# Output projection of a decoder layer: plain float32 products replaced by three products of high and low parts, with split weights stored in DRAM and streamed back

## The chip, the cores and the metric

One core of a Trainium2 chip runs one program. The metric is the device time of one execution in microseconds. The engines are TensorE (PE, with its weight loads as PEld), VectorE (DVE), ScalarE (ACT), GpSimd (POOL) and SyncE (SP), which here issues nearly all DMAs.

## What is computed

Two decoder layers on 1040 tokens (16 meta tokens and 1024 others) of width 1024. The part that matters is the mixer of layer 0. It has eight heads of sparse attention (each query keeps 256 keys) and eight heads of a gated linear recurrence. Their outputs are put side by side and mapped by one matrix:

```
o = jnp.concatenate([o_a.reshape(B, L, A_WIDTH), o_b.reshape(B, L, B_VAL_WIDTH)], axis=-1)
return o @ w_out
...
h = layer_norm(ALPHA * h + mix, ln_mix_g[layer], ln_mix_b[layer])
```

`o` is 1040 x 1024 and `w_out` 1024 x 1024, both float32.

## The kernel before

The program has three stages with a barrier after each: `projection` (to about 464 us), `mixers` (to about 937 us) and `trunk` (the rest: both feed-forward parts, the pooling mixer, the norms).

**Projection.** Most products of this kernel are already made from parts: a float32 operand is rounded to the type float32r (the high part, by ACT), the rest (the low part, by POOL or DVE) is a second float32r tensor, and low x high, high x low and high x high are summed in PSUM. `w_in` comes in twelve slabs of 256 columns. ACT makes `slabH`, POOL makes `slabL` (`split`, L374), PE runs 24 matmuls for each output unit (L498, L501), and ACT takes the unit out of its bank (`out_of_bank`). Slabs 0 and 1 fill gaps of the score computation; slabs 2 to 11 follow. Beside them DVE and ACT search the top 256 keys, and POOL, after its last slab, makes the distances for which DVE then waits. The order of all this is one list, `order`, walked by every engine.

**Mixers.** There are nine tiles m = 0 to 8, the first of 16 tokens, the others of 128. Each tile has eight steps h = 0 to 7, one for each attention head and for one level of the recurrence; after tile 8 come eight steps of m = 9 and six of m = 10 for what is left over. Every engine walks the same list `steps`. On PE a step is, in this order: the logits of head h (`qk`, L1246; it needs the maximum of the head before, `nmax`, from DVE), one level product (`gram`, L1289; it needs POOL's `carry` of the level before, L1124 and L1128), one job on the bank SHARED (`shared_job`), the transposes of the probabilities of the head before (L1303), their product with the values (L1314), and at some steps a quarter of an output projection (`out_job`, `quarter`, L1239). The jobs on SHARED, at steps 0 to 6, are: meta, out, kT, state, qa, ot_att, ot_rec. kT transposes the keys of the recurrence, and ACT copies them to `k_tok` (L1439), after the exponential of the step (L1372) and two gate functions (L1402, L1404). ot_att and ot_rec transpose the outputs of attention and recurrence; ACT copies them to `oT` (L1454, L1450). All users of SHARED follow each other in one count: each waits until the one before has been taken out (`shared_done`).

A quarter is the product of a tile of `oT` with 256 columns of `w_out`: eight plain float32 matmuls, which the chip runs as 16. Its weights lie in `w_out_part`, two halves of 512 KB, each with one buffer. SP asks for the next first half when PE has read the present one (`wq_read`) and for the next second half when the quarter is complete (`load_w`, L1005). DVE adds the result to `y` (`out_added`, L1595). The quarters 0 to 3 of tile t run at (t+1, 7), (t+2, 1), (t+2, 3) and (t+2, 5):

```
jobs = {7: (m - 1, 0), 1: (m - 2, 1), 3: (m - 2, 2), 5: (m - 2, 3)}
```

The last six quarters (two of tile 7 and all of tile 8) take their weights from four 1 MB loads into `kaT` and `va`, which are free at the end (`kept_quarter`, L1046). Those of tile 8 use four banks of their own. DVE finishes the recurrence's output `on` with two products at step 4 (L1635, L1638).

Of the kernel before, what the change touches and what calls it, by code (L numbers as in the profile page):

```python
# [5 lines left out]
F32 = mybir.dt.float32  # L6
# [26 lines left out]
PG = D // len(POOL_WINDOWS)  # L33

# [49 lines left out]
def build(nc, ins, out):  # L84
# [3 lines left out]
    with ExitStack() as top:  # L88
# [21 lines left out]

        banks = top.enter_context(nc.psum_tensor("banks", [P, 8, 512], F32))
# [9 lines left out]
        with ExitStack() as heads:  # L121
            with ExitStack() as mixer:

                score = (y[:, :, :].rearrange("p m d -> p (m d)")[:, NT * D - SC_LAST:NT * D],
                         last_draw)
                kiT = sb(mixer, "kiT", [P, 2, P])
                masks = kiT[:, :, :].rearrange("p a t -> p (a t)").bitcast(U8).rearrange("p (l t) -> p l t", t=P)
                w_qa0 = y[:, 2, :].rearrange("p (k f) -> p k f", k=QC)
                kaT = sb(mixer, "kaT", [P, 4, L])
                va = sb(mixer, "va", [P, NT, A_WIDTH])  # L130
                with stage() as c:
                    projection(nc, c, sem, sb, banks, ident, x, meta, w_in_v, ins, score, cqT, kaT, va, y, qz_dram, vg_dram, kiT, masks, w_qa0)
                with stage() as c:
                    mixers(nc, c, sem, sb, banks, ident, x, meta, ins, score, masks, w_qa0, cqT, kaT, va, y, qz_dram, vg_dram, raw, draw)
            hH = sb(top, "hH", [P, DC, L], F32R)
            hL = sb(top, "hL", [P, DC, L], F32R)
# [4 lines left out]
def projection(nc, c, sem, sb, banks, ident, x, meta, w_in_v, ins, score, cqT, kaT, va, y, qz_dram, vg_dram, kiT, masks, w_qa0):  # L141
# [26 lines left out]
    slab_in_va = va[:, :, :].rearrange("p m f -> p (m f)")[:, 0:2 * SLAB].rearrange("p (s k f) -> p s k f", s=2, k=DC)  # L168

# [45 lines left out]
    dist_done, placed = sem("dist_done"), sem("placed")  # L215
    stored = [sem(f"stored{i}") for i in range(NS)]
# [43 lines left out]

    def slab_part(n):
# [46 lines left out]
    def _(sp):  # L308
        for m, (t0, n) in enumerate(TILES):
# [12 lines left out]
            if m == 2:  # L322
# [8 lines left out]
                sp.dma_start(w_qi[:, :, :], ins["w_uq_idx"][0].rearrange("(k p) f -> p k f", p=P)).then_inc(w_qi_loaded, 16)  # L331
        for j, (col, _, _, _) in enumerate(SLABS):
# [5 lines left out]
            if j == len(SLABS) - 2:  # L338
                sp.wait_ge(sc_psum, len(units))
            sp.dma_start(slab_raw(j), w_in_v[:, :, col:col + SW]).then_inc(slab_loaded[j % 2], 16)  # L340
            if j == len(SLABS) - 2:
                sp.dma_start(w_qa0, ins["w_uq"][0].rearrange("(k p) f -> p k f", p=P)).then_inc(w_qa_loaded, 16)

    @block.gpsimd
    def _(pool):
# [39 lines left out]
        for what, m, *part in order:  # L385
# [15 lines left out]
            elif what == "low":  # L401
                split(m)
                splits += 1
        pool.wait_ge(qi_psum, 2 * NQ)
# [102 lines left out]
    def _(act):  # L507
# [35 lines left out]
        for what, m, *part in order:  # L543
            if what == "split":
                split(m)
            if what == "out":
# [245 lines left out]
def mixers(nc, c, sem, sb, banks, ident, x, meta, ins, score, masks, w_qa0, cqT, kaT, va, y, qz_dram, vg_dram, raw, draw):  # L792
# [44 lines left out]
    oT = sb(c, "oT", [P, 2, DC, P])  # L837
    QW = D // 4
    wq = sb(c, "w_out_part", [P, 2, DC // 2, QW])
# [19 lines left out]
    op_psum, op_added = sem("op_psum"), sem("op_added")  # L859
# [26 lines left out]
    def out_job(m, h):  # L886

        jobs = {7: (m - 1, 0), 1: (m - 2, 1), 3: (m - 2, 2), 5: (m - 2, 3)}
# [4 lines left out]

    def kept_quarter(t, q):

        return t == NT - 1 or (t == NT - 2 and q in LAST_ORDER[0:2])
# [60 lines left out]

    block = c.enter_context(nc.Block())

    @block.sync  # L960
    def _(sp):
# [36 lines left out]
        def load_w(job):  # L998
            for kh in range(2):
# [4 lines left out]
                q = job % 4  # L1004
                sp.dma_start(wq[:, kh, :, :], w_v[:, kh * 4:kh * 4 + 4, q * QW:(q + 1) * QW]).then_inc(wq_loaded[kh], 16)  # L1005

# [20 lines left out]
        for m, h in steps:  # L1027
# [143 lines left out]
    def _(pe):  # L1171
# [56 lines left out]
        def quarter(m, q, bank):  # L1228
            n = TILES[m][1]
            for k in range(DC):  # L1230
                if kept_quarter(m, q):
                    w = wq_last[q][:, k, :]
                    if k == 0:
                        pe.wait_ge(wl_loaded[q], 16)
                else:
                    w = wq[:, k // 4, k % 4, :]
                    if k % 4 == 0:
                        pe.wait_ge(wq_loaded[k // 4], 16 * (4 * m + q + 1))
                last = nc.tensor.matmul(banks[0:n, bank, 0:QW], oT[:, m % 2, k, 0:n], w, start=(k == 0), stop=(k == DC - 1))  # L1239
# [123 lines left out]
    def _(act):  # L1363
# [59 lines left out]
        def off_shared(what, m):  # L1423
# [25 lines left out]
            if what == "ot_rec":  # L1449
                ins_ = nc.scalar.activation(oT[:, m % 2, 4:8, 0:n], four(src)[:, :, P - n:P], ACT.Copy)  # L1450
            if what == "ot_att":
                if m >= 2:
                    act.wait_ge(shared_psum, nth["op", m - 2, 3])
                ins_ = nc.scalar.activation(oT[:, m % 2, 0:4, 0:n], four(src)[:, :, 0:n], ACT.Copy)  # L1454
# [32 lines left out]
    def _(dve):  # L1487
# [111 lines left out]

        gates(0, 4)  # L1600
        nc.vector.memset(S[:], 0.0).then_inc(dve_pads, 1)
        for i, (m, h) in enumerate(steps):
# [11 lines left out]
            if 1 <= i <= NU:  # L1614
                turned(i - 1)
            if out_job(m, h):
# [817 lines left out]
```

## Time and profile before

| | us |
|---|---|
| median of 3 runs (lowest, highest) | 2550.95 (2549.44, 2551.99) |
| the profiled execution, its own time | 2547.58 |
| its span, first to last instruction | 2545.9 |
| PE busy | 2469.9 (97%) |
| DVE, ACT, POOL busy | 1114.2, 950.1, 1062.1 |
| mean granted TensorE clock | 0.992 of full speed |

The profiled execution took 1.7 us more than its span. Busy time of PE says that matmuls were under way, not that they ran at their fastest, since they overlap; the start of one instruction to the start of the next tells what one costs. An idle time in brackets stands before an instruction and names what ended it.

### The profile page before, as it was taken

To read this page: it belongs to the slowest core of one execution; us is meant where nothing else is said; L and a number is where in the kernel's file an instruction comes from. 1 tells how busy PE (TensorE), PEld (TensorE's weight loads), DVE (VectorE), ACT (ScalarE), POOL (GpSimd) and SP (SyncE) were. 2 spreads that over 40 slices of the span, in tenths; PEclk is the share of its full clock that TensorE was granted. 3 is DMA by queue.
4 is the path that set the end of the run, shared out by engine and by line. 5 is a ranking of instruction groups with operands and counts; after the bars stand their busy time and mean duration, and the time that the engine had idled before them with its cause. 6 is when DMAs were issued, how large, how long until landed. Compare 5 with 4: busy or idle time off the path is not lost.

```text
span 2545.9 us, 36095 instructions
## 1 busy us (share of the span) xinstructions
PE 2469.9 (97%) x14044; PEld 2129.0 (84%) x14044; DVE 1114.2 (44%) x2233; ACT 950.1 (37%) x1609; POOL 1062.1 (42%) x617
## 2 busy tenths in 40 slices
PE   7999999899999989999999999999999999999997
PEld 7889999768888778899898888888888888888885
DVE  7798986444554523333333332333323322232224
ACT  3687783334443224222223332323333322332222
POOL 1434213365554224444433544544434443455342
PEclk9999999899999999999999999999999999999998
DMA  4101230333332333333323323333233233333431
GB/s 139 34 18 56 79 103 24 108 112 110 113 106 90 93 116 109 96 96 105 89 74 99 99 75 93 88 112 97 70 99 100 67 116 99 100 89 110 116 94 47
DMA packets 275002, 231.43 MB, mean 91 GB/s; under 512 B 10768, under 2 KB 255568, under 8 KB 274832
## 3 DMA queue, kind: packets, MB, share of 16 engines
q1 hardware_dynamic: 266640, 220.59, 29.1%
q10 hardware_dynamic: 8192, 8.52, 1.0%
q8 instruction: 113, 1.85, 0.3%
q14 instruction: 57, 0.47, 0.1%
HBM read 215.81 MB, written 12.71 MB: 90 GB/s over the span
## 4 chain that ended last, share of the span: by engine, by line
PE 60%; ACT 1%; DVE 1%; DMA 1%; POOL 0%; issue 0%; POOLq 0%; SPq 0%; ACTq 0%; DVEq 0%
PE banks L2067 38%; PE banks L2101 19%; PE banks L2137 1%; PE banks L2115 1%; PE banks L1764 1%; PE banks L2124 1%; PE banks L2092 0%; PE banks L2095 0%; DMA last_draw<-in_w_down 0%; DMA cq_raw<-in_w_up 0%; POOL dL L1985 0%; POOL wL L1978 0%; DVE y L2318 0%; ACT dH L2187 0%; ACT hH L1774 0%
## 5 line engine op out<-in xcount | busy, mean ns | idle before, releaser
L1978 POOL TENSOR_TENSOR wL<-cq_raw,wH 128x2048 fp32r<-128x2048 f32 x87 | 407.0, 4678 | 531.5 <-ACT wH L2181 531.5
L2067 PE MATMUL banks<-hL,wH 128*128 128x512 f32 (+1 forms) x1760 | 618.7, 352 | 6.6 <-ACT hid L2196 3.8
L2067 PE MATMUL banks<-hH,wL 128*128 128x512 f32 (+1 forms) x1760 | 617.9, 351 | 0.0
L2067 PE MATMUL banks<-hH,wH 128*128 128x512 f32 (+1 forms) x1760 | 616.2, 350 | 0.0
L2292 DVE TENSOR_TENSOR hid<-hid,banks 128x512 f32<-128x512 f32 (+1 forms) x110 | 64.4, 585 | 729.4 <-PE banks L2067 629.0
L2067 PEld LDWEIGHTS banks<-hL,wH 128*128 128x128 f32 x1760 | 331.3, 188 | 55.8 <-ACT hid L2196 5.1
L2067 PEld LDWEIGHTS banks<-hH,wL 128*128 128x128 f32 x1760 | 331.2, 188 | 46.3
L2067 PEld LDWEIGHTS banks<-hH,wH 128*128 128x128 f32 x1760 | 331.8, 188 | 45.0
L1985 POOL TENSOR_TENSOR dL<-last_draw,dH 128x1024 fp32r<-128x1024 f32 x88 | 220.9, 2510 | 321.3 <-ACT dH L2187 321.2
L2318 DVE TENSOR_TENSOR y<-y,banks 128x512 f32<-128x512 f32 (+1 forms) x340 | 232.3, 687 | 195.0 <-PE banks L2101 194.0
L2187 ACT ACTIVATE dH<-last_draw 128x1024 fp32r<-128x1024 f32 x88 | 93.3, 1061 | 517.6 <-PE banks L2101 340.7
L2101 PE MATMUL banks<-dH,hidL 128*128 128x512 f32 x704 | 279.2, 397 | 2.3 <-issue 2.3
L2101 PE MATMUL banks<-dL,hidH 128*128 128x512 f32 x704 | 278.0, 395 | 0.0
L2101 PE MATMUL banks<-dH,hidH 128*128 128x512 f32 x704 | 277.5, 394 | 0.0
L2198 ACT ACTIVATE hidH<-hid 128x512 fp32r<-128x512 f32 (+1 forms) x110 | 60.4, 549 | 382.1 <-DVE hid L2292 382.1
L2181 ACT ACTIVATE wH<-cq_raw 128x2048 fp32r<-128x2048 f32 x87 | 166.0, 1908 | 40.1 <-DMA cq_raw<-in_w_up 37.8
L2101 PEld LDWEIGHTS banks<-dH,hidL 128*128 128x128 f32 x704 | 132.3, 188 | 35.0 <-issue 2.7
L2101 PEld LDWEIGHTS banks<-dH,hidH 128*128 128x128 f32 x704 | 132.6, 188 | 31.5
L1124 POOL TENSOR_TENSOR qp<-qp,tot 64x256 f32<-64x256 f32 x112 | 80.6, 720 | 186.9 <-PE banks L1289 182.5
L2101 PEld LDWEIGHTS banks<-dL,hidH 128*128 128x128 f32 x704 | 132.6, 188 | 30.5
L501 PE MATMUL banks<-shared,hH 128*128 128x256 f32 (+1 forms) x648 | 136.9, 280 | 0.0
L501 PE MATMUL banks<-shared,hL 128*128 128x256 f32 (+1 forms) x432 | 120.7, 280 | 0.0
(279 smaller groups left out, 4124.4 us busy)
## 6 DMA issues: line engine op xcount, KB each, us to landing
cq_raw<-in_w_gate SPq DMA_DIRECT2D x88, 512.0 KB, 4.5
cq_raw<-in_w_up SPq DMA_DIRECT2D x88, 512.0 KB, 6.0
last_draw<-in_w_down SPq DMA_DIRECT2D x88, 512.0 KB, 3.4
w_out_part<-in_w_out SPq DMA_DIRECT2D x60, 512.0 KB, 3.9
va<-in_w_in SPq DMA_DIRECT2D x10, 1024.0 KB, 5.4
va<-in_x SPq DMA_DIRECT2D x8, 512.0 KB, 4.3
vg_scratch<-y ACTq DMA_DIRECT2D x32, 128.0 KB, 1.7
y<-in_x SPq DMA_DIRECT2D x8, 512.0 KB, 7.5
```

The lines of the kernel that those rows point to most:

```text
L501: last = nc.tensor.matmul(banks[0:n, bank, 0:SW], h[:, k, a:a + n], w[:, k, :], start=first, stop=stop)
L1124: nc.gpsimd.tensor_tensor(late, late, blocks[r, :, 0, :].to_broadcast([HD, n, 2 ** l]), ALU.mult)\
L1764: last = self.nc.tensor.transpose(self.banks[:, self.bank_of(i), k * P:k * P + n], self.y[0:n, m, kk * P:(kk + 1) * P], self.ident[0:n, 0:n])
L1978: nc.gpsimd.tensor_tensor(wL[:, ff % 2, :, :, :].rearrange("p g k f -> p (g k f)"), raw[:, :, :, :].rearrange("p g k f -> p (g k f)"), wH[ ...
L1985: nc.gpsimd.tensor_tensor(dL[:, ff % 2, :], draw, dH[:, ff % 2, :].bitcast(F32), ALU.subtract)\
L2067: last = nc.tensor.matmul(banks[:, GU + (2 * q + g) % 3, 0:n], wt[:, ff % 2, g, k, :], h[:, k, a:a + n], start=(k == 0 and part == 0), sto ...
L2101: last = nc.tensor.matmul(banks[0:n, DN + num % 3, :], h[:, (2 * g + u) % 3, t0 - ph.t0:t0 - ph.t0 + n], wt[:, u, (j % 2) * 512:(j % 2 + 1 ...
L2181: nc.scalar.activation(wH[:, ff % 2, :, :, :], raw[:, :, :, :], ACT.Copy).then_inc(w_hi, 2)
L2187: nc.scalar.activation(dH[:, ff % 2, :], draw, ACT.Copy).then_inc(d_hi, 1)
L2198: nc.scalar.activation(hidH[:, ff % 3, a - ph.t0:a - ph.t0 + n], hid[:, q % 2, 0:n], ACT.Copy)\
L2292: nc.vector.tensor_tensor(hid[:, q % 2, 0:n], hid[:, q % 2, 0:n], banks[:, GU + (2 * q + 1) % 3, 0:n], ALU.mult)\
L2318: nc.vector.tensor_tensor(at, at, banks[0:n, DN + num % 3, :], ALU.add).then_inc(y_added, 1)
```

## The change

The quarters of tiles 0 to 7 become three float32r products for each of the eight pieces: 24 matmuls. Only tile 8 stays plain. The copy of `oT` becomes `oH` by ACT and `oL` by DVE (`o_low`), both with one buffer. In the projection stage eight pieces of `w_out` (512 KB each) are loaded, split by ACT (128 x 1024) and POOL, and both parts are written to the DRAM tensor `w_out_split` in pieces of 1 MB; SP issues this beside slabs 5 to 9. The mixers stream 1 MB for each half, for all 32 quarters. The quarters move to the steps 7, 1, 2 and 4. `oT` of tile 8 lies in `probs`.

```diff
@@ projection, order list
+    OUT_WITH = 5
+    split_after = [first_unit[OUT_WITH - 3 + c // 2] + 2 + c % 2 * 2 for c in range(len(OUT_CHUNKS))]
...
         if k == DC - 1:
             order.append(("out", u))
+            if u in split_after:
+                order.append(("w_out", split_after.index(u)))
@@ projection, SP
+        def load_out(c):
+            q, kh = OUT_CHUNKS[c]
+            if c >= 2:
+                sp.wait_ge(wo_stored[c % 2], 16 * (c // 2))
+            sp.dma_start(out_part(c)[:, 1, :].rearrange("p (k f) -> p k f", k=DC // 2),
+                         w_out_v[:, 4 * kh:4 * kh + 4, q * QW:(q + 1) * QW]).then_inc(wo_loaded[c % 2], 16)
+
+        def store_out(c):
+            q, kh = OUT_CHUNKS[c]
+            sp.wait_ge(wo_lo, c + 1)
+            sp.dma_start(wo_dram[q, kh], out_part(c)).then_inc(wo_stored[c % 2], 16)
...
             if j == len(SLABS) - 2:
-                sp.wait_ge(sc_psum, len(units))
+                for i in range(2):
+                    sp.wait_ge(wo_stored[i], 16 * len(OUT_CHUNKS) // 2)
             sp.dma_start(slab_raw(j), w_in_v[:, :, col:col + SW]).then_inc(slab_loaded[j % 2], 16)
...
+            for c in range(2 * (j - OUT_WITH) - 2, 2 * (j - OUT_WITH)):
+                if 0 <= c < len(OUT_CHUNKS):
+                    store_out(c)
+                if j >= OUT_WITH and c + 2 < len(OUT_CHUNKS):
+                    load_out(c + 2)
@@ mixers
-    oT = sb(c, "oT", [P, 2, DC, P])
-    wq = sb(c, "w_out_part", [P, 2, DC // 2, QW])
+    oH = sb(c, "oH", [P, DC, P], F32R)
+    oL = sb(c, "oL", [P, DC, P], F32R)
+    wq = sb(c, "w_out_part", [P, 2, 2, DC // 2, QW], F32R)
+    oT_last = probs[:, :, 0:DC // 2 * P].rearrange("p a (k t) -> p a k t", k=DC // 2)
...
-        jobs = {7: (m - 1, 0), 1: (m - 2, 1), 3: (m - 2, 2), 5: (m - 2, 3)}
+        jobs = {7: (m - 1, 0), 1: (m - 2, 1), 2: (m - 2, 2), 4: (m - 2, 3)}
@@ mixers, SP
-                sp.dma_start(wq[:, kh, :, :], w_v[:, kh * 4:kh * 4 + 4, q * QW:(q + 1) * QW]).then_inc(wq_loaded[kh], 16)
+                sp.dma_start(wq[:, kh, :, :, :].rearrange("p a k f -> p a (k f)").bitcast(F32), wo_dram[job % 4, kh]).then_inc(wq_loaded[kh], 16)
...
-                if t < NT - 1 and 4 * t + q + 1 < 4 * (NT - 1) - 2:
+                if 4 * t + q + 1 < 4 * (NT - 1):
                     load_w(4 * t + q + 1)
@@ mixers, PE, quarter
+                for part, (o, w) in enumerate(((oL, 0), (oH, 1), (oH, 0))):
+                    last = nc.tensor.matmul(banks[0:n, bank, 0:QW], o[:, k, 0:n], wq[:, k // 4, w, k % 4, :],
+                                            start=(k == 0 and part == 0), stop=(k == DC - 1 and part == 2))
@@ mixers, ACT, off_shared
+                    if m:
+                        act.wait_ge(shared_psum, nth["op", m - 1, 3])
+                    nc.scalar.activation(oH[:, 4 * half:4 * half + 4, 0:n], o_columns(what, n), ACT.Copy).then_inc(o_hi, 1)
@@ mixers, DVE
+        def o_low(what, m):
...
+            dve.wait_ge(o_hi, 2 * m + half + 1)
...
+            nc.vector.tensor_tensor(oL[:, at, 0:n], o_columns(what, n), oH[:, at, 0:n].bitcast(F32), ALU.subtract)\
+              .then_inc(shared_done, 1)
```

The instructions move at three places. First PE at tile 7, steps 2 to 4, before (L1193 is kT, L1196 state, L1185 qa):

```order
L1193 MATMUL banks<-ident,key 128x128 x4
L1303 MATMUL banks<-ident,probs 128x128 x7
L1314 MATMUL banks<-va,pT 128x64 x7
L1246 MATMUL banks<-kaT,qaT 128x512
L1246 MATMUL banks<-kaT,qaT 128x400
L1289 MATMUL banks<-qp,key 128x128 x4
L1196 MATMUL banks<-vt,k_tok 128x128 x4
L1303 MATMUL banks<-ident,probs 128x128 x7
L1314 MATMUL banks<-va,pT 128x64 x7
L1239 MATMUL banks<-w_out_part,oT 128x256 x8
```

and the same place now (every line number of this part is 46 to 48 higher; the quarter is L1286):

```order
L1239 MATMUL banks<-ident,key 128x128 x4
L1351 MATMUL banks<-ident,probs 128x128 x7
L1362 MATMUL banks<-va,pT 128x64 x7
L1286 MATMUL banks<-w_out_part,oL 128x256
L1286 MATMUL banks<-w_out_part,oH 128x256 x2
...
L1294 MATMUL banks<-kaT,qaT 128x512
L1294 MATMUL banks<-kaT,qaT 128x400
L1337 MATMUL banks<-qp,key 128x128 x4
L1242 MATMUL banks<-vt,k_tok 128x128 x4
```

The quarter stood behind the state job, a step later; now it is the next user of SHARED behind kT.

Then DVE at tile 8, steps 4 to 6, now (L1648 is `out_added`, L1698 and L1701 finish `on`, L1562 the maxima, L1658 the new low part):

```order
L1648 SCALAR_TENSOR_TENSOR y<-y,banks 128x256
L1698 TENSOR_TENSOR on<-on,rsh 128x512
L1701 TENSOR_TENSOR on<-on,gt 128x512
L1562 ISA probs,nmax<-banks,last_draw 128x1024
...
L1585 COPY pT<-banks 128x512
L1658 TENSOR_TENSOR oL<-banks,oH 128x512
L1736 BN_STATS n_bn<-y 128x6
L1737 BN_STATS n_bn<-y 128x6
```

Before, `out_added` of the last quarter stood at the place of the first L1658, a step later, and DVE had no low parts to make.

Last, SP at the end of the mixers, before and now:

```order
L1046 DMA kaT<-in_w_out 128x8x256 x2
L1046 DMA va<-in_w_out 128x8x256 x2
L1058 DMA last_draw<-in_w_down 128x1024
```

```order
L1051 DMA w_out_part<-w_out_split 128x2048 x2
L1092 DMA kaT<-in_w_out 128x8x256 x2
L1051 DMA w_out_part<-w_out_split 128x2048 x2
L1092 DMA va<-in_w_out 128x8x256 x2
L1051 DMA w_out_part<-w_out_split 128x2048 x2
L1104 DMA last_draw<-in_w_down 128x1024
```

Two pairs of streamed halves now stand between and behind the loads of the last tile's weights.

## Rows read from the trace of the kernel before

**Rows 1.** The page's busy time, and busy time in a stretch of the mixers.
```profile
PE 2469.9 (97%) x14044; PEld 2129.0 (84%) x14044; DVE 1114.2 (44%) x2233; ACT 950.1 (37%) x1609; POOL 1062.1 (42%) x617
...
600.00:700.00 100.00, 99.82 (x675) 86.94 (x674) 51.82 (x107) 41.23 (x104) 54.11 (x70) 1.00 0.38 116
```
**Rows 2.** Timeline of PE, tile 5, steps 1 to 4: start, length, engine, line, instruction.
```profile
670.99 3.62 PE L1239 MATMUL banks<-w_out_part,oT 128*128 128x256 f32 x16
674.44 1.27 PE L1246 MATMUL banks<-kaT,qaT 128*128 128x512 f32 x4
...
678.50 1.32 PE L1246 MATMUL banks<-kaT,qaT 128*128 128x512 f32 x4
...
683.35 3.67 PE L1239 MATMUL banks<-w_out_part,oT 128*128 128x256 f32 x16
686.85 1.27 PE L1246 MATMUL banks<-kaT,qaT 128*128 128x512 f32 x4
```
**Rows 3.** Timeline of ACT in the projection: copies that follow a unit of 24 products.
```profile
417.66 0.38 ACT L526 ACTIVATE va<-banks 128x256 f32<-128x256 f32 x1 [2.44 <-PE banks L501]
420.50 0.38 ACT L526 ACTIVATE va<-banks 128x256 f32<-128x256 f32 x1 [2.46 <-PE banks L501]
```
**Rows 4.** Timeline of ACT, tile 5, step 2: gate functions, then the keys.
```profile
678.93 0.61 ACT L1402 ACTIVATE u<-zt 128x512 f32<-128x512 f32 x1
...
680.11 0.58 ACT L1439 ACTIVATE k_tok<-banks 128x512 f32<-128x512 f32 x1
```
**Rows 5.** Timelines of PE and ACT: the same place in tiles 2 and 7.
```profile
538.27 0.68 PE L1246 MATMUL banks<-kaT,qaT 128*128 128x272 f32 x2
539.46 0.58 ACT L1439 ACTIVATE k_tok<-banks 128x512 f32<-128x512 f32 x1
...
789.23 1.75 PE L1246 MATMUL banks<-kaT,qaT 128*128 128x512 f32 x4
790.23 0.58 ACT L1439 ACTIVATE k_tok<-banks 128x512 f32<-128x512 f32 x1
```
**Rows 6.** PE's waits in step 3: tile 2's product, and the waits list, 480 to 940.
```profile
539.99 1.13 PE L1289 MATMUL banks<-qp,key 128*128 128x128 f32 x8 [1.04 <-POOL key L1128]
...
PEld banks L1196 <- ACT k_tok L1439: 1.1, 3, 0.5
```
**Rows 7.** Timelines of POOL (tile 5) and DVE (tile 5, and the end).
```profile
694.54 1.72 POOL L1124 TENSOR_TENSOR qp<-qp,tot 64x256 f32<-64x256 f32 x2
...
693.42 1.64 DVE L1638 TENSOR_TENSOR on<-on,gt 128x512 f32<-128x512 f32 x1
...
917.22 0.69 DVE L1638 TENSOR_TENSOR on<-on,gt 128x512 f32<-128x512 f32 x1
```
**Rows 8.** The page's DMA issues (size, median to landing), and the landings of kaT.
```profile
last_draw<-in_w_down SPq DMA_DIRECT2D x88, 512.0 KB, 3.4
w_out_part<-in_w_out SPq DMA_DIRECT2D x60, 512.0 KB, 3.9
va<-in_w_in SPq DMA_DIRECT2D x10, 1024.0 KB, 5.4
...
DMA to landing us min/median/max: 6.7/7.9/9.1
```
**Rows 9.** Timeline of PE at the end of the mixers.
```profile
906.34 3.62 PE L1239 MATMUL banks<-w_out_part,oT 128*128 128x256 f32 x16
910.54 3.72 PE L1239 MATMUL banks<-kaT,oT 128*128 128x256 f32 x16 [0.58 <-DVE y L1595]
...
917.00 3.72 PE L1239 MATMUL banks<-kaT,oT 128*128 128x256 f32 x16 [1.50 <-ACT oT L1454]
921.31 0.66 PE L1217 MATMUL banks<-ident,on 128*128 128x128 f32 x4 [0.58 <-DVE y L1595]
922.65 7.17 PE L1239 MATMUL banks<-kaT,oT 128*128 128x256 f32 x32 [0.69 <-ACT oT L1450]
```
**Rows 10.** Timeline of DVE in the projection, after its search.
```profile
422.11 1.03 DVE L755 TENSOR_SCALAR_CACHE_REDUCE search_rows<-y,found 128x784 f32<-128x784 f32 x1 [19.70 <-POOL y L409]
```

More of the change, by code:

```diff
@@ L33 @@
 PG = D // len(POOL_WINDOWS)
+QW = D // 4
+OUT_CHUNKS = [(q, kh) for q in range(4) for kh in range(2)]
 COL_CQ, COL_KA, COL_VA = 0, Q_RANK, Q_RANK + A_WIDTH
@@ L403, in _ @@
                 splits += 1
+            elif what == "w_out":
+                pool.wait_ge(wo_hi, m + 1)
+                low = out_part(m)[:, 1, :]
+                nc.gpsimd.tensor_tensor(low.bitcast(F32R), low, out_part(m)[:, 0, :], ALU.subtract).then_inc(wo_lo, 1)
         pool.wait_ge(qi_psum, 2 * NQ)
@@ L545, in _ @@
                 split(m)
+            if what == "w_out":
+                act.wait_ge(wo_loaded[m % 2], 16 * (m // 2 + 1))
+                nc.scalar.activation(out_part(m)[:, 0, :].bitcast(F32R), out_part(m)[:, 1, :], ACT.Copy).then_inc(wo_hi, 1)
             if what == "out":
@@ L789, in _, with mixers @@
         linked(nc.vector.tensor_scalar(masks[:, LEVELS, :], xor, 0.0, None, ALU.is_equal))
-def mixers(nc, c, sem, sb, banks, ident, x, meta, ins, score, masks, w_qa0, cqT, kaT, va, y, qz_dram, vg_dram, raw, draw):
+def mixers(nc, c, sem, sb, banks, ident, x, meta, ins, score, masks, w_qa0, cqT, kaT, va, y, qz_dram, vg_dram, wo_dram, raw, draw):
     W = 4 * P
@@ L956, in four, with o_columns @@
         return ap.rearrange("p (f t) -> p f t", f=4)
+    def o_columns(what, n):
+        return four(banks[:, SHARED, :])[:, :, P - n:P] if what == "ot_rec" else four(banks[:, SHARED, :])[:, :, 0:n]
     block = c.enter_context(nc.Block())
@@ L1448, in off_shared @@
                 ins_ = nc.scalar.activation(on[:, :], src, ACT.Copy)
[L1449 to L1454, printed above, removed]
+            if what in ("ot_att", "ot_rec"):
+                half = what == "ot_rec"
+                if m == NT - 1:
+                    act.wait_ge(meta_kept, NU)
+                    act.wait_ge(t_psum, turned_to(NU - 1))
+                    ins_ = nc.scalar.activation(oT_last[:, half, :, :], four(src), ACT.Copy)
+                else:
+                    if m:
+                        act.wait_ge(shared_psum, nth["op", m - 1, 3])
+                    nc.scalar.activation(oH[:, 4 * half:4 * half + 4, 0:n], o_columns(what, n), ACT.Copy).then_inc(o_hi, 1)
+                    return
             ins_.then_inc(shared_done, 1)
@@ L1598, in out_added @@
                 dve.wait_ge(shared_done, nth["op", m, 3])
+        def o_low(what, m):
+            n = TILES[m][1]
+            half = what == "ot_rec"
+            dve.wait_ge(o_hi, 2 * m + half + 1)
+            at = slice(4 * half, 4 * half + 4)
+            nc.vector.tensor_tensor(oL[:, at, 0:n], o_columns(what, n), oH[:, at, 0:n].bitcast(F32), ALU.subtract)\
+              .then_inc(shared_done, 1)
         gates(0, 4)
@@ L1615, in _ @@
                 turned(i - 1)
+            if shared_job(m, h) and shared_job(m, h)[0] in ("ot_att", "ot_rec") and m < NT:
+                o_low(*shared_job(m, h))
             if out_job(m, h):
```

35 lines of the change are left out of this document (20 added, 15 removed).

## The prediction

> **What bounds the kernel now.** Read the page first: PE is busy for 97% of the span, and in the middle of the mixers for 99.8 of 100 us, while DVE and POOL are at half [rows 1]. That alone doesn't say that shorter products shorten the stage, so the timeline of PE comes next. In tile 5 each step starts where the one before ends, with no idle time to speak of [rows 2]: there PE's own work sets the pace. The second thing to see is how late the others run behind it. ACT finishes k_tok at 680.69, when PE has been in the next step since 678.50 [rows 2, 4]. That lateness is free now, because PE first needs k_tok after its logits and level product of step 3. The third view is the end of the mixers, where PE waits between quarters [rows 9] and loads stand behind each other [rows 8].
>
> **The product itself.** A plain quarter takes from 670.99 to 674.44, 3.45 us, and at step 3 from 683.35 to 686.85, 3.50 us [rows 2]; I take 3.45. A unit of 24 float32r products of the same shape, 128 x 256, takes 420.50 − 417.66 = 2.84 us in the projection [rows 3]. So a quarter loses 0.61 us. 28 quarters lie before the end piece, which is worked out by itself: 28 x 0.61 = **−17.1 us**, if PE keeps the pace.
>
> **The move of quarter 2 to step 2.** It now stands directly behind kT on SHARED and can't start before k_tok is copied. The copy comes late for a reason that the change leaves alone: it starts from quarter 1 of the same tile, after which DVE adds, normalizes and takes the maximum, and ACT does the exponential, two gates, then the copy [rows 4]. In tile 5 PE arrives at the quarter at 678.50 and the copy ends at 680.69, 0.07 us of signal more: 2.26 us of wait. In tile 2 it is 540.04 against 538.27, 1.84 us; in tile 7 790.81 against 789.23, 1.65 us [rows 5]. The three between (3, 4, 6) read 2.34, 2.35 and 1.95 in the same way. Six tiles: **+12.4 us**. In tile 8 the copy comes in time, since PE there waits for DVE anyway. Something comes back: behind this wait PE no longer waits in step 3 for POOL (1.04 us in tile 2) or for k_tok (1.1 us in three places) [rows 6], nor for some 0.25 us of others: **−2.4 us**. The bounds are 0 (were PE to arrive as late as the copy) and the full 12.4.
>
> **The low part and DVE's queue.** `o_low` is one DVE instruction of 128 x 512, twice a tile, 0.69 us by the nearest row of that size, 917.22 [rows 7]. DVE has room on average, but look at what is queued behind one wait: at step 4 `out_added` now waits for quarter 3, and behind it stand the two products on `on`, the maximum of step 5, the low part, four statistics instructions and the maximum of step 6, while PE has two steps without a quarter (692.24 − 686.85 = 5.4 us was step 4; a step without special jobs in tile 5 is 678.50 − 674.44 = 4.1 us [rows 2]). From the end of quarter 3 DVE needs 0.3 + 0.3 + 1.3 to 2.9 + 1.0 + 0.6 + 0.2 + 0.7 + 1.7 + 0.8 = 6.9 to 8.5 us before the maximum of step 6 is there; PE wants it after two steps, at 8.2 us. The spread is `on`: 1.64 us for one product beside POOL, 0.69 us alone [rows 7]. POOL is likely idle at that moment now, because it had all of quarter 3 to finish. I take +0.4 us a tile, 7 tiles, **+3 us**, with the ends 0 and 1.5 us a tile (10 us). The Trainium skill (SBUF — State Buffer, "SBUF: two separate sides") says that a DVE instruction with two SBUF inputs and a GpSimd instruction exclude each other for a whole instruction. By that rule the doubling is a wait for POOL, the trace agrees, and this term would be near its low end where POOL is idle.
>
> **Short steps.** Steps 3 and 5 lose their quarter. POOL needs 1.72 us for the first two instructions of a level [rows 7] and 0.63 for the third, so a step must be about 3.3 us or PE waits at its level product, as it does in tile 2 [rows 6]. In tiles 2 and 3 steps 3 and 5 fall to some 2.5 to 3.6 us. With the copies of qa before quarter 3, **+2 us** (0 to 4).
>
> **Weights.** Each half is now 1 MB. A 1 MB load landed after 5.4 us; 512 KB after 3.9 with rows of 1 KB and 3.4 with rows of 4 KB [rows 8]. The new pieces are rows of 8 KB, so I take 4.7 for one and 2.7 more for one queued behind (the two kaT loads, issued 0.5 us apart, landed 2.4 us apart after issue, 2.9 us apart in time [rows 8]). The tight place is quarter 1 to 2. The first half is asked for 1.4 us before quarter 1 ends and lands 3.3 us after its end; the second lands about 6 us after its end. PE wants them at 2.6 + 1.8 = 4.4 us and 5.9 us in tile 2 and later in the others. The wait for k_tok covers them: **+0.5 us**. If that cover were gone, they would cost about what it costs. The Trainium skill (DMA: Bandwidth & Descriptors, "Measured") gives 6.15 us for 1 MB; by it tile 2 alone would wait longer, and the end piece below would be some 3 us longer. The row of 5.4 us is this kernel's, so it is preferred.
>
> **The end.** Before, quarters 2 and 3 of tile 7 had kept weights; they ran at 910.54 and 917.00, the second behind ot_att, and the last four quarters began at 922.65 [rows 9]. Now (9,1), (9,2) and (9,4) hold nothing on PE but three quarters, each needing a fresh pair of 1 MB halves in buffers that are just being read, and two pairs of 1 MB loads share the queue. By the rates above: quarter 1 ends near 908.5. Its successor's first half is asked for at 907.1, behind two kaT loads that now end near 908.2, and lands at 911.7, the second at 914.5: quarter 2 ends at 915.9. The va pair, issued meanwhile, is through at 920.3; the halves of quarter 3 follow at 923.0 and 925.6, and it ends at 927.0. Then ot_att and ot_rec, one after the other, each with a transpose of 0.66, a copy and 0.6 us of waits: 3.5 us. The last four quarters start at 930.5 instead of 922.65: **+7.9 us** (5 to 11).
>
> **The projection stage.** Eight ACT copies (half of a slab's 1.9 us each) and eight POOL subtractions (half of 4.6 us) are added, and sixteen DMAs on SP. The ACT copies, and whatever they cost DVE, fall on the search, which ends 19.7 us before POOL lets DVE go on [rows 10]; PE's output banks are eight deep. SP's new waits (for the low part, for a store) lie about a slab ahead of the next slab load. I cost it at **0**; without that cover the copies would cost up to 8 us.
>
> Sum: −17.1 + 12.4 − 2.4 + 3 + 2 + 0.5 + 7.9 = **+6.3 us**. On the profiled execution's 2547.6 this is 2553.9; that execution lies 3.4 us under the median, so I forecast 2550.95 + 6.3 = **2557 us**.
>
> **Rivals.** (1) *The waits are mostly absorbed, the product wins.* PE's wait at step 2 gives DVE, ACT and POOL a lead, and later waits vanish: half of the 12.4 is paid, no DVE or short-step term, end +5: −17.1 + 6.2 − 2.4 + 5 = −8, 2543 us. For it: DVE and POOL are half idle. Against: the bracketed waits of PE that could vanish are few. (2) *Everything small comes out well but the two big waits stay*: −17.1 + 12.4 − 2.4 + 7.9 = +0.8, 2552 us, no change. (3) *Weights become the bound at quarter 2.* Loads in company took 6.7 to 9.1 us [rows 8]. From a second half that lands more than 5.9 us (tile 2) to 8.2 us (tile 7) after quarter 1's end, PE waits for it instead of k_tok; at 9.1 us this adds 3.2, 1.9, 1.6, 1.4, 1.1, 0.9: +10 us, 2567 us. Against: little other traffic stands at step 1. (4) *The split isn't hidden in the projection*: SP, blocked on a store, delays a slab, or ACT's copies delay a unit: +8 us, 2565 us. Against: the slack above.
>
> **Numbers.** The measurement tells about 0.2%, 5.1 us, from no change. Forecast and its neighbourhood (2553 to 2561): 0.4; rival 2: 0.2; rival 1: 0.2; rival 3: 0.12; rival 4: 0.08. Faster by over 0.2% (under 2545.9) is rival 1 and a little: 0.2. Rival 2 and the lower third of the forecast give no change (to 2556.1): 0.33. The rest is slower: 0.47. The range takes in rival 1's time and ends at rival 3's: 2543 to 2567.
>
> **What would show it.** Right: quarters of 2.8 us on PE; a wait of about 2 us before quarter 2 in tiles 2 to 7, ended by ACT's k_tok; two gaps of several us, ended by DMAs into w_out_part, before the second and third of the three quarters near 910; the projection's end still at 464. Wrong: gaps before quarter 2 ended by w_out_part (rival 3), a later barrier (rival 4), PE waits for DVE's maxima at steps 6 and 7 much over 0.4 us a tile, or quarters that take over 3 us, which would take away the gain on which all of it stands.

## The result, and the profile after

The change makes the kernel slower: 2575.1 us median (2571.19 to 2576.3, 4 runs) against 2550.26 (2549.44 to 2551.99, 4 runs), a ratio of 1.0094 with a 95% interval of 1.0078 to 1.0110. That is +24.8 us where +6.3 was forecast, and above the upper end of the range. The two profiled spans are 2574.6 and 2545.9 us, mean granted clock 0.983 and 0.992.

The page of the changed kernel, busy time and DMA issues, and two stretches, of which the second answers to [rows 1]:

```profile
PE 2468.5 (96%) x14300; PEld 2144.0 (83%) x14300; DVE 1121.2 (44%) x2249; ACT 955.7 (37%) x1617; POOL 1078.6 (42%) x625
...
w_out_part<-w_out_split SPq DMA_DIRECT2D x64, 1024.0 KB, 5.3
...
va<-in_w_in SPq DMA_DIRECT2D x10, 1024.0 KB, 5.9
w_out_split<-slab_last SPq DMA_DIRECT2D x8, 1024.0 KB, 8.6
...
slab_last<-in_w_out SPq DMA_DIRECT2D x8, 512.0 KB, 4.2
```
```profile
300.00:400.00 100.00, 92.39 (x726) 90.30 (x726) 79.36 (x232) 77.07 (x141) 27.11 (x8) 0.97 0.41 135
600.00:700.00 100.00, 94.90 (x713) 85.19 (x712) 48.61 (x108) 39.53 (x102) 52.98 (x70) 0.96 0.54 195
```

The first of these windows lies in the projection, and read before the change:

```profile
300.00:400.00 100.00, 100.00 (x830) 97.99 (x829) 82.23 (x248) 78.80 (x150) 18.49 (x4) 1.00 0.25 82
```

PE is busy 1.4 us less than before in a span that is 28.7 us longer: PE is idle for longer, in the projection and in the mixers. The clock column fell too, from 1.00 to 0.97 and 0.96, so part of the busy time is at half speed and hides how much shorter the products have become. Over the whole trace the granted clock is at half (1.2 GHz) for 45 us before and for 89 us now.

**Where the 28.7 us lie.** DVE's first instruction of the mixers marks the end of the projection. Before:

```profile
464.62 0.48 DVE L1495 MEMSET key<- 128x512 f32 x1 [11.37 <-PEq L101]
```

and now:

```profile
479.30 0.48 DVE L1548 MEMSET key<- 128x512 f32 x1 [10.34 <-PEq L103]
```

The mixers begin 14.7 us later. POOL's first mask instruction, which stands ahead of everything that the change adds, already starts at 199.91 us where it was 196.48; so 3.4 of the 14.7 us are of this execution's start, and 11.3 of the projection. For the rest each trace is divided at three marks (the first quarter, the end of tile 7's quarter 1, the start of the last four quarters), with the time that the clock was at half:

| us | before | changed |
|---|---|---|
| start of the mixers, less what the start is late | 464.6 | 475.9 |
| first quarter to the end of tile 7's quarter 1 | 390.5 | 390.9 |
| of it with PE idle | 7.5 | 20.5 |
| of it with the clock at half | 0 | 14 |
| from there to the last four quarters | 12.7 | 24.6 |
| mixers as a whole | 473.9 | 485.1 |

**The projection** has three waits on PE where there was none. Two are shown; the third, 2.23 us before 345.84, is again for ACT's `y`. Behind the second and the third the clock is at 1.2 GHz, for 3.4 us each, from 333 and from 347:

```profile
315.39 0.29 PE L544 MATMUL banks<-shared,hL 128*16 128x256 f32 x1 [1.65 <-POOL shared L421]
...
333.37 0.55 PE L544 MATMUL banks<-shared,hL 128*128 128x256 f32 x1 [3.73 <-ACT y L581]
```

The waits come to 7.6 us, and 6.8 us at half clock can cost 3.4 more: together 11.0 of the 11.3 us. ACT, which drains PE's banks, waits for the raw pieces of `w_out` (the list of waits, and one row of the three that are over 7 us; the fourth is 1.94):

```profile
ACT slab_last L591 <- DMA slab_last<-in_w_out: 24.7, 4, 7.8
```
```profile
298.01 1.06 ACT L591 ACTIVATE slab_last<-slab_last 128x1024 fp32r<-128x1024 f32 x1 [7.51 <-DMA slab_last<-in_w_out]
```

And why the pieces are late can be read on SP, with the first low part on POOL beside it:

```profile
229.22 0.37 SPq L372 DMA_DIRECT2D va<-in_w_in  x1
229.64 1.12 SPq L355 DMA_DIRECT2D slab_last<-in_w_out  x2
253.75 0.37 SPq L372 DMA_DIRECT2D va<-in_w_in  x1
254.16 0.58 SPq L361 DMA_DIRECT2D w_out_split<-slab_last  x1
262.81 0.37 SPq L355 DMA_DIRECT2D slab_last<-in_w_out  x1
```
```profile
237.44 2.40 POOL L446 TENSOR_TENSOR slab_last<-slab_last 128x1024 fp32r<-128x1024 f32 x1 [8.29 <-ACT slab_last L591]
```

The low part is ready at 239.84. Its store is issued at 254.16: in SP's program it stands behind the next slab's load, and that waits for both parts of an earlier slab, of which POOL's low part (`slab_lo`) comes last, at 253.68. The next piece may be loaded when the store has landed, 8.6 us later, at 262.81, and it takes 4.4 us more. The store also shares the queue with the 1 MB slab load that was issued 0.4 us ahead of it; experiment 2 shows what it takes without that. Two pieces a slab go through this, and ACT's own queue holds the copies of the pieces between the copies that free PE's banks.

**The middle.** The quarter is nearly as short as forecast. Quarter 0 of a tile, at step 7, took from 655.85 to 659.36 before, 3.51 us:

```profile
655.85 3.67 PE L1239 MATMUL banks<-w_out_part,oT 128*128 128x256 f32 x16
659.36 1.27 PE L1246 MATMUL banks<-kaT,qaT 128*128 128x512 f32 x4
```

The same quarter now takes from 673.55 to 676.50, 2.95 us, so 0.56 less. And the wait for k_tok stands where it was forecast:

```profile
673.55 0.36 PE L1286 MATMUL banks<-w_out_part,oL 128*128 128x256 f32 x1
...
676.50 1.26 PE L1294 MATMUL banks<-kaT,qaT 128*128 128x512 f32 x4
...
693.99 1.23 PE L1362 MATMUL banks<-va,pT 128*128 128x64 f32 x10
697.29 0.39 PE L1286 MATMUL banks<-w_out_part,oL 128*128 128x256 f32 x1 [2.08 <-ACT k_tok L1487]
```

PE's waits from 480 to 965:

```profile
PE banks L1286 <- ACT k_tok L1487: 11.5, 6, 2.2
PE banks L1286 <- DMA w_out_part<-w_out_split: 11.3, 3, 6.5
PE banks L1337 <- POOL key L1174: 8.4, 9, 1.6
PE banks L1294 <- DVE nmax L1562: 6.9, 11, 1.3
```

Before, the last two lines read 7.5 us (7 times) and 7.4 (11 times).

What the shorter products gave can be read from PE's busy time in the middle, from the first quarter to the end of tile 7's quarter 1, which holds 30 quarters. The lines are of before, of the changed kernel, and of experiment 3, in which the clock never falls in this stretch (length, PE busy, clock):

```profile
519.38:909.95 390.57, 383.03 (x2554) 1.00 0.36 111
532.97:923.87 390.90, 370.41 (x2796) 0.98 0.53 186
536.14:915.20 379.06, 365.80 (x2796) 1.00 0.55 192
```

At full clock PE is busy 17.2 us less than before, 0.57 us a quarter. In the changed kernel 4.6 us of that are taken back by the stretches at half clock (by their length, 13 us of them with PE busy, it could be up to 6.4), and PE is idle 13.0 us longer.

**The end.** PE at the place of [rows 9], and SP there:

```profile
927.96 0.55 PE L1286 MATMUL banks<-w_out_part,oL 128*128 128x256 f32 x1 [4.07 <-DMA w_out_part<-w_out_split]
...
940.36 0.55 PE L1286 MATMUL banks<-w_out_part,oL 128*128 128x256 f32 x1 [6.47 <-DMA w_out_part<-w_out_split]
...
948.50 7.17 PE L1280 MATMUL banks<-kaT,probs 128*128 128x256 f32 x32 [0.69 <-ACT probs L1502]
```
```profile
910.63 1.76 SPq L1051 DMA_DIRECT2D w_out_part<-w_out_split  x2
912.49 2.60 SPq L1092 DMA_DIRECT2D kaT<-in_w_out  x2
922.49 1.77 SPq L1051 DMA_DIRECT2D w_out_part<-w_out_split  x2
924.31 1.68 SPq L1092 DMA_DIRECT2D va<-in_w_out  x2
930.89 3.37 SPq L1051 DMA_DIRECT2D w_out_part<-w_out_split  x2
```

Ten loads of 1 MB in a row, and the DMA engines never idle (columns: PE, PEld, DVE, ACT, POOL, clock, DMA share, GB/s):

```profile
920.00:925.00 5.00, 3.89 (x28) 3.21 (x26) 1.00 (x2) 0.00 (x0) 0.00 (x0) 1.00 1.11 349
925.00:930.00 5.00, 2.04 (x9) 2.07 (x10) 1.36 (x3) 0.00 (x0) 3.34 (x2) 0.72 0.98 352
930.00:935.00 5.00, 3.79 (x17) 3.20 (x15) 1.00 (x2) 0.00 (x0) 0.00 (x0) 0.60 1.07 359
935.00:940.00 5.00, 0.00 (x0) 0.00 (x0) 0.18 (x2) 0.42 (x2) 0.00 (x0) 0.74 1.05 412
```

The two kaT loads landed after 10.0 and 12.4 us, for [rows 8]'s 6.7 and 9.1. The clock column is well below 1 in three of the four windows: the quarters between the waits run partly at 1.2 GHz.

### The profile page after: what moved, and what is told of

The parts are those of the page before. It is cut to its first block, busy times and chain, and to the rows that moved or that the text cites. A ratio compares the mean times of both kernels' runs of the same rounds, so it can differ in the third digit from the quotient of the medians.

```text
span 2574.6 us, 36676 instructions
## 1 busy us (share of the span) xinstructions
PE 2468.5 (96%) x14300; PEld 2144.0 (83%) x14300; DVE 1121.2 (44%) x2249; ACT 955.7 (37%) x1617; POOL 1078.6 (42%) x625
## 4 chain that ended last, share of the span: by engine, by line
PE 59%; DMA 1%; ACT 1%; POOL 1%; DVE 1%; issue 0%; POOLq 0%; SPq 0%; ACTq 0%; DVEq 0%
PE banks L2130 37%; PE banks L2164 19%; PE banks L2200 1%; PE banks L2178 1%; PE banks L1827 1%; PE banks L2187 1%; DMA last_draw<-in_w_down 0%; PE banks L2155 0%; PE banks L2158 0%; POOL dL L2048 0%; DMA cq_raw<-in_w_up 0%; POOL wL L2041 0%; ACT dH L2250 0%; DVE y L2381 0%; ACT hH L1837 0%
```

## The experiments

Nine kernels in three batches, each batch with its own runs of the kernel before on the same chip (medians 2549.93, 2549.82 and 2549.39 us). Ratios are against these; a difference from the changed kernel is one of medians, and its 4 runs were in a batch of their own. What the code lines show as taken out is the changed kernel's.

### 1. The split in the projection alone

The mixers of the kernel before, behind the projection of the changed one: the parts are made and stored, and nobody reads them.

```
-        jobs = {7: (m - 1, 0), 1: (m - 2, 1), 2: (m - 2, 2), 4: (m - 2, 3)}
+        jobs = {7: (m - 1, 0), 1: (m - 2, 1), 3: (m - 2, 2), 5: (m - 2, 3)}
...
-                for part, (o, w) in enumerate(((oL, 0), (oH, 1), (oH, 0))):
-                    last = nc.tensor.matmul(banks[0:n, bank, 0:QW], o[:, k, 0:n], wq[:, k // 4, w, k % 4, :],
+                last = nc.tensor.matmul(banks[0:n, bank, 0:QW], oT[:, m % 2, k, 0:n], w, start=(k == 0), stop=(k == DC - 1))
```

> Before, plus the projection part of the change alone: w_out is loaded, split and stored, but the mixers of before run unchanged and do not read it. Theory A (the trace after: barrier at 479.1 instead of 464.4, of which 3.3 us are already there at 200 us, ahead of the first new instruction): the split costs about 11 us, 2561 us, with the barrier near 475. Theory M (the projection's part is a fluke of one execution and the loss is in the mixers): 2550 us, within 3 us.

Measured: 2559.27 us (2553.98 to 2563.58, 6 runs), ratio 1.0034 (1.0022 to 1.0047). ACT's waits for the pieces are 24.6 us in 4 times, as in the changed kernel, PE's three 7.6 us together, and the clock is at half twice for 3.4 us. The projection is 11.2 us longer than before (start of the mixers at 478.09, of which 2.3 are the start's).

So 9.3 of the 24.8 us are paid before the first short product runs.

### 2. Stores and loads of pieces ahead of the slab's wait

In SP's program the stores and loads of pieces now stand in front of the waits for `slab_hi` and `slab_lo`; the slab's load is behind them.

```
+            for c in range(2 * (j - OUT_WITH) - 2, 2 * (j - OUT_WITH)):
+                if 0 <= c < len(OUT_CHUNKS):
+                    store_out(c)
+                    if c + 2 < len(OUT_CHUNKS):
+                        load_out(c + 2)
...
                 sp.wait_ge(slab_hi, j - 1)
                 sp.wait_ge(slab_lo, j - 1)
```

> The change, with SP's stores and following loads of w_out pieces moved ahead of the wait for the next slab's split, so that they go out when the low part is done. Theory A1 (ACT stands for a piece that SP asked for too late, 7.4 to 7.8 us three times): the three waits go, the barrier comes about 11 us earlier, 2564 us. Rival A2 (the added work itself costs it: eight ACT copies of 1.06 us, eight POOL subtractions of 2.4 us, and DVE beside them): no gain, 2575 us.

Measured: 2565.71 us (2562.33 to 2566.65), ratio 1.0059 (1.0044 to 1.0074), 9.4 us under the changed kernel. SP and the start of the mixers in it:

```profile
239.81 0.34 SPq L361 DMA_DIRECT2D w_out_split<-slab_last  x1
246.19 0.37 SPq L355 DMA_DIRECT2D slab_last<-in_w_out  x1
246.67 0.45 SPq L361 DMA_DIRECT2D w_out_split<-slab_last  x1
253.41 0.37 SPq L355 DMA_DIRECT2D slab_last<-in_w_out  x1
```
```profile
467.98 0.48 DVE L1551 MEMSET key<- 128x512 f32 x1 [11.43 <-PEq L103]
```

The store leaves at 239.81, when the low part is there, and not at 254.16. The eight stores also land sooner, the changed kernel's first and this one's second:

```profile
DMA to landing us min/median/max: 6.2/8.6/11.1
DMA to landing us min/median/max: 4.1/4.3/6.7
```

So half of the 8.6 us is not the store's own: most of the stores now go out when no slab load has just been issued. With 3.3 us of late start taken off, the mixers begin at 464.7, as before, and PE's three waits are gone: all eight copies, eight subtractions and sixteen DMAs are now hidden. So it was not their work that cost the 11 us but the place of the stores behind SP's waits and beside the slab loads; the two were moved together, and how the 11 us divide between them isn't shown.

### 3. Quarter 2 back at step 3

```
-        jobs = {7: (m - 1, 0), 1: (m - 2, 1), 2: (m - 2, 2), 4: (m - 2, 3)}
+        jobs = {7: (m - 1, 0), 1: (m - 2, 1), 3: (m - 2, 2), 4: (m - 2, 3)}
```

> The change, with quarter 2 back at step 3 and quarter 3 left at step 4. Theory B (quarter 2 stands for k_tok at step 2, 11.8 us in six tiles): these waits go, weights have time enough, 9 to 12 us faster than the change, 2564 us. Rival B2 (PE's wait at step 2 is only time that POOL or DVE would take from it anyway): under 3 us faster, 2572 us or more. Rival B3 (quarters at neighbouring steps 3 and 4 stand for their weights or for the copy of qa instead): no gain.

Measured: 2562.21 us (2556.87 to 2565.76), ratio 1.0046 (1.0028 to 1.0064), 12.9 us under the changed kernel. The 11.5 us of waits for k_tok are gone and no window between 520 and 900 us has a clock below 1. From the first quarter to the end of tile 7's quarter 1 it takes 379.1 us, 11.8 less than the changed kernel and 11.4 less than the kernel before. Of the 11.8 us, 7.2 are idle time of PE and 4.6 are busy time at the lower clock. Some waits for the loads come up, 3.6 us in four places.

### 4. The loads into `va` asked for last

SP asks for the last two quarters' weights of tile 8 only behind the halves of tile 7's quarter 3.

```
-            if m == NT and h in (0, 2):
-                for q in LAST_ORDER[h:h + 2]:
+            if (m, h) == (NT, 0):
+                for q in LAST_ORDER[0:2]:
...
+            if (m, h) == (NT, 2):
+                sp.wait_ge(pv_done, turned_to(NU - 1))
+                for q in LAST_ORDER[2:4]:
+                    sp.dma_start(wq_last[q], w_v[:, :, q * QW:(q + 1) * QW]).then_inc(wl_loaded[q], 16)
```

> The change, with the two 1 MB loads into va asked for after the streamed halves of quarter 3 of tile 7 instead of before. Theory C (queue order: the last streamed halves lie behind 2 MB that nobody needs yet): quarter 3 ends 5 to 6 us earlier, 2569 us. Rival C2 (the latency of a buffer that is refilled only when it has been read bounds both quarters, whatever stands in the queue): no gain, 2575 us. Rival C3 (the last tile then waits for va): slower.

Measured: 2568.73 us (2565.13 to 2575.0), ratio 1.0082 (1.0063 to 1.01), 6.4 us under the changed kernel, but the interval overlaps the changed kernel's (1.0078 to 1.0110), so this gain is not clear of noise. In the trace the stretch from tile 7's quarter 1 to the last four quarters only falls from 24.6 to 22.1 us. Its waits fell by more, from 10.5 us to 3.93 + 0.86 + 1.05 + 0.95 = 6.8, but the clock is now at half without a break from 919.9 to 937.0, 17.1 us where it was 13.6, and the quarters between the waits take longer by it. Its projection, which the edit doesn't touch, was 1.2 us shorter in the profiled execution. The order of the loads is a small part of the end.

### 5. The last two quarters of tile 7 plain, from kept weights

```
-                if 4 * t + q + 1 < 4 * (NT - 1):
+                if 4 * t + q + 1 < 4 * (NT - 1) - 2:
...
+                if kept_quarter(m, q):
+                    if k == 0:
+                        pe.wait_ge(wl_loaded[q], 16)
+                    last = nc.tensor.matmul(banks[0:n, bank, 0:QW], four((qt, zt)[k // 4][:, :])[:, k % 4, :], wq_last[q][:, k, :],
...
+                        nc.scalar.activation(four((qt, zt)[half][:, :]), four(src), ACT.Copy)
```

> The changed kernel, but quarters 2 and 3 of tile 7 are plain products from weights kept in kaT, as before; ACT writes plain copies of tile 7's outputs for them, and SP streams two quarters less. In its place stand two plain quarters for two split ones: +1.2 us. Theory A (the end piece loses its time to pairs of 1 MB loads that can't land in a quarter, and to the half clock that follows those waits): both waits on w_out_part after 920 us of the changed kernel (4.1 and 6.5 us) are gone, the last four quarters start 9 to 12 us nearer to the start of the mixers than 469.2 us, and the time falls by 8 to 12 us, to about 2565. Theory B (those waits only uncover what DVE, POOL and ACT need for ot_att and ot_rec anyway): the waits on the loads go but come back before the last four quarters, ended by DVE or ACT, and the time falls by 0 to 4 us.

Measured: 2565.06 us (2557.77 to 2566.35), ratio 1.0057 (1.0044 to 1.007), 10.0 us under the changed kernel. The end in its trace:

```profile
921.40 1.99 PE L1290 MATMUL banks<-kaT,qt 128*128 128x256 f32 x8 [0.58 <-DVE y L1663]
...
932.74 7.17 PE L1284 MATMUL banks<-kaT,probs 128*128 128x256 f32 x32 [0.69 <-ACT probs L1512]
```

Both waits on the loads are gone, and the mark-to-mark stretch is 11.9 us, which is less than the 12.7 of before. So nothing else stood behind those waits: DVE and ACT end only waits of under 0.8 us there, and POOL none.

### 6. Stores early and quarter 2 at step 3

> Two repairs together: quarter 2 at step 3 of the next tile but one, as before, and SP's stores and loads of the weight pieces ahead of the wait for the slab's high part. If the parts are additive, the time is the changed kernel's less 9.4 us (the stores alone) and less 12.9 us (the step alone): about 2553, which is the time before within 4 us. If the leads share something (the clock's half-speed stretches, or the end of the mixers, where both queue for the same loads), one of them is worth less together: 2556 to 2560.

Measured: 2547.99 us (2544.25 to 2551.74, 12 runs), ratio 0.9993 (0.9984 to 1.0002): as fast as before, and just under the 2553 within 4 us that parts which add up were to give. Against the changed kernel it is −27.1 us, where the two repairs by themselves gave −9.4 and −12.9. There is no sign that they share anything. The 4.8 us that it is better than their sum are no finding either: they are less than the spread of the changed kernel's 4 runs (5.1), and of the 26.6 us between the two profiled spans 6.0 lie in the start and the trunk, which neither edit touches.

### 7. All three repairs

> All three repairs: quarter 2 at step 3, stores early, and the two kept plain quarters at the end of tile 7. What is left is the shorter product: 26 quarters at 0.61 us, 15.9 us, less whatever short steps, w_out waits in the middle and a changed queue cost. Theory A (the product keeps what the trace of one quarter says): 2538 to 2545, faster than both kernels. Theory B (with quarters 17% shorter PE runs into DVE, POOL and the loads at every step, so that most of the gain is absorbed even with the three losses undone): 2548 to 2553, no change from before.

Measured: 2536.69 us (2533.01 to 2539.82, 5 runs), ratio 0.9949 (0.9937 to 0.9961). It is faster than both kernels, by 13.1 us than the one before, and a little under the range of theory A. Windows, waits and the end:

```profile
300.00:400.00 100.00, 100.00 (x827) 97.99 (x826) 83.50 (x250) 82.97 (x155) 21.51 (x7) 1.00 0.35 116
600.00:700.00 100.00, 98.23 (x763) 87.89 (x762) 53.68 (x120) 42.45 (x106) 55.50 (x74) 1.00 0.58 204
```
```profile
PE banks L1350 <- POOL key L1181: 9.1, 9, 1.6
PE banks L1299 <- DMA w_out_part<-w_out_split: 2.8, 4, 0.9
```
```profile
908.20 7.17 PE L1287 MATMUL banks<-kaT,probs 128*128 128x256 f32 x32 [0.69 <-ACT probs L1515]
```

Mark to mark: the middle takes 377.6 us (390.5 before, −12.9), the end 11.9 (12.7 before), the mixers 458.2 (473.9 before, −15.7), and the projection what it took before. The other 2.0 of the 15.7 us lie ahead of the first quarter, where nothing is new and the clock was at half for 3.3 us less; they are not the product's.

The expectation counts 26 short quarters. There are 32 in the changed kernel (64 loads of halves) and 30 here, all in the middle: at 0.61 us they were worth 18.3 us. In the middle PE is busy 17.8 us less than before and idle 4.9 us more: 2.8 for the loads, 1.6 more for POOL's `key`, 1.0 for the copies of qa, less some small ones. So about 5 of some 18 us are absorbed.

### 8. k_tok copied ahead of the exponential

Quarter 2 stays at step 2; ACT makes the copy before it waits for the maximum.

```
-            early = shared_job(m, h) if h in (3, 5) else None
+            early = shared_job(m, h) if h in (2, 3, 5) else None
```

> The changed kernel with one line different: ACT copies kT to k_tok ahead of the exponential and the gates of step 2, not behind them; quarter 2 stays at step 2. Theory A (the copy is late only by its place in ACT's queue: in tile 5 of the changed kernel kT is through on PE at 693.6 us, ACT idles until 694.64 for the maximum, and copies at 696.66): the copy ends near 694.2, before PE arrives at 695.2, the 12.3 us of waits for k_tok are gone, and with them the half-clock stretches between 590 and 900 us; the time falls as far as it did with the quarter at step 3, to 2561 to 2564. Theory B (the wait only changes its name: SHARED free earlier, but the exponential behind the copy is later, so that PE waits for the probabilities, or quarter 2's loads, landing 6 us after quarter 1, now show): the time falls by 0 to 6 us, to 2569 to 2575.

Measured: 2566.41 us (2557.82 to 2570.4, 6 runs), ratio 1.0059 (1.0044 to 1.0073), 8.7 us under the changed kernel, between the two theories' ranges. The waits for k_tok are gone, and this list of PE's waits from 480 to 900 us says what came in their place:

```profile
PE banks L1286 <- DMA w_out_part<-w_out_split: 9.6, 8, 1.9
```

It was 0.7 us there in the changed kernel. At step 2 the second pair of halves has one step to land in, and the wait for k_tok had hidden that it is late. From mark to mark the middle is 384.6 us, 6.3 less than in the changed kernel. PE's waits for k_tok and the loads together fell only from 12.2 to 9.6 us; the time at half clock fell from 14 to 3.4 us. Of the 6.3 us, 2.6 are idle time of PE and 3.7 busy time.

Which wait is followed by a slow stretch can't be told from its length. Here, after waits of 0.6 to 1.9 us, it was one tile of six. After the waits for k_tok, of 1.5 to 2.2 us and the same in four traces, it was three of six in the changed kernel, five in experiments 2 and 4, and four in experiment 5.

### 9. The three repairs, with the early copy in place of step 3

The kernel of experiment 7 with quarter 2 at step 2 and experiment 8's line.

> The kernel with all three repairs, but quarter 2 at step 2 again with the early copy of k_tok in place of the move to step 3. Theory A (place and copy are two ways to the same thing): within 4 us of 2536.7. Theory B (at step 2 the second pair of halves has only one step to land in, where before a wait of 2 us on k_tok covered it): waits on w_out_part of 1 to 3 us in each of six tiles, 2545 to 2555.

Measured: 2544.67 us (2539.34 to 2552.41, 11 runs), ratio 0.9978 (0.9969 to 0.9987), 8 us slower than experiment 7, just under theory B's range and outside theory A's. The waits on the loads are back: 10.2 us on PE from 480 to 900, 7 times, up to 1.9. Its profiled execution (2550.7 us) also has a stretch of some 10 us at half clock near 842 us with no wait of PE over 0.5 us ahead of it, of which the other traces have none; its marks are therefore not compared.

## Why the prediction was wrong

By the steps of the prediction, with trace numbers where the medians don't divide so finely:

- **"The projection stage ... I cost it at 0": the step that failed.** It cost 11.3 us in the trace and 9.3 in runs (experiment 1). The reason given, that SP's waits lie "about a slab ahead", looked at how far away they are and not at the order in which SP reaches them. A store that was ready stood 14.3 us behind a slab load and then took 8.6 us to land beside it (4.3 when it goes out early), and the next piece's load needed that landing. Rival 4 named the place and about the size (+8 us), if with another order: not a slab stood for a store, but the stores stood for a slab, and ACT, standing for the pieces, delayed units. Its chance of 0.08 was too low, on the argument of "the slack above": DVE's 19.7 us [rows 10] are slack of DVE, while PE in the projection has none, as 100.00 of 100 us busy from 300 to 400 would have said.
- **The clock: a term that was left out.** Nothing in the sum prices what follows a wait. The clock is at half for 44 us more than before in the trace. In the middle, where the busy times can be compared, this cost 4.6 us, and in the projection up to 3.4 of the 11.3.
- **"The end, +7.9": right mechanism, mis-sized.** Both gaps stood where they were foretold, with 4.07 and 6.47 us. The term sets off 1.4 us for the short quarters 0 and 1 of tile 7, which the table counts in the middle. From the end of quarter 1 the text has 22.0 us (908.5 to 930.5), +9.3; it measured 24.6, +11.9, and taking it out gave back 10.0 in runs. What was short is the queue: ten loads kept it full from 911 on, and the kaT pair took 3.3 us longer each than [rows 8]; and the quarters between the waits ran partly at 1.2 GHz. The prediction said that by the 6.15 us for 1 MB in the Trainium skill (DMA: Bandwidth & Descriptors, "Measured") the end would be some 3 us longer. The end came out longer by 2.6, but this does not bear that figure out: the page gives it for loads issued by GpSimd, as the busy time of the DMA engines, while here the halves' median from issue to landing over the run is 5.3 us, nearer to the row of 5.4. At the end it is the company that makes it 7.2.
- **"The move of quarter 2, +12.4": right.** Measured 11.5 us on PE in six tiles. Of the way back, −2.4, the rows that it names are gone from the lists (POOL's 1.04 us in tile 2 and the 1.1 us for k_tok in step 3).
- **"The product, −17.1": right.** With the two quarters that the end term holds, 30 were priced at 18.3 us; at full clock they gave 17.2, 0.57 us each for 0.61.
- **"DVE's queue, +3": not there.** PE's waits for `nmax` went from 7.4 to 6.9 us. The spread was `on`, and the low end of it came true: its second product takes 0.69 us now (median of 9), where it took 1.64 before, as the text foresaw for an idle POOL. 0 was the value to take. **"Short steps, +2"**: waits for POOL's `key` rose by 0.9 us, or 1.6 in experiment 7.
- **"Weights, +0.5 ... if that cover were gone, they would cost about what it costs"**: right, and shown by experiment 8: 0.7 us under the cover, 9.6 without it.
- **The middle as a whole** came near by luck. Its terms give −2.8, with the two quarters of tile 7, and it measured +0.4. The product gave 1.1 us too little and the clock took 4.6, but PE's idle time rose by only 13.0 us where 15.5 were priced (+12.4 −2.4 +3 +2 +0.5).
- **Start and trunk**, 3.4 and 2.8 of the 28.7 us of span, hold nothing new. The trunk took from 1605.6 to 1610.2 us in the eleven traces, so its 2.8 us are within scatter. Ahead of 200 us the clock is at half for 3.4 us in the trace of before and for 10.2 in the changed kernel's, which is worth up to 3.4 us. But the ten traces with the new projection code all start 1.2 to 3.9 us later than the one of before, two of them with as little time at half clock, so whether the program has a part in it stays open.

Of the 18.5 us that the forecast missed, 9.3 are the projection (runs). By the trace the middle missed by 3.2 us and the end by 2.6. The remaining 3 to 4 us lie among start, trunk and the scatter of executions, and are not settled.

## What to carry to other kernels

A step that is "hidden" has to be followed through the program of the queue that issues it: list what stands ahead of each new DMA on its engine and what that waits for, then add the store's landing, in the company that it will have, before a buffer is loaded again. In a stage where PE is busy for all of a window, slack of DVE is none. Before splitting operands in two, count the megabytes where the loads already stand in a queue, since there the shorter product meets a transfer that is twice as long, and keep the plain form for those few products: 30 of 32 short quarters stay short, and the kernel is 13.1 us faster than before. And a wait may cover another one: ask what arrives next before pricing its removal. A wait can also cost more than its length, since the clock may be at half behind it: compare busy times between kernels only where the clock column is the same.

## What the runs showed of the hardware

- A store of 1 MB from SBUF to DRAM landed after 8.6 us (median of 8) in the changed kernel, where half of the stores were issued 0.4 us behind a 1 MB load, and after 4.3 us (median of 8, 4.1 to 6.7) in experiment 2, where most were issued alone. Loads of 1 MB landed after 5.3 us (64) and 5.9 (10) in the changed kernel, the fastest after 4.7, and after 10.0 and 12.4 us as the third and fourth of four issued within 2.3 us.
- The granted clock fell to 1.2 GHz for some 3.4 us, or twice that, after some of the waits of 1.5 to 2.2 us that PE had once a tile, between stretches in which it was busy: in three tiles of six, and in five, four and five of six in experiments 2, 5 and 4. Without these waits it stayed at 2.4 GHz from 520 to 900 us (experiments 3, 6 and 7). Around the waits of 4 and 6.5 us at the end it was at half for 14 us in total. In one execution it fell with no wait over 0.5 us just ahead of it.
- A DVE product of two tiles in SBUF (`on`, 128x512) took 1.64 us (median of 9) before and 0.69 us in the changed kernel, where quarter 3 now stands ahead of it and POOL was idle beside it at 716.08 us, in tile 5.
